# One ring of weight blocks for the last four stages of a hybrid decoder step, the merge's branch products in three passes, and a transposed down projection

## The reference, cut to what matters

```python
h  = RMSNorm(x) * (1 + scale1(c)) + shift1(c)
P  = h @ w_in                      # RWKV-7 group | NSA group | gates gA, gB
yA = RWKV7(P_rwkv) @ w_pa ;  yB = NSA(P_nsa) @ w_pb        # (T, 512) @ (512, 1024)
x  = x + gate1(c) * ((sigmoid(gA) * yA + sigmoid(gB) * yB) @ w_o)
h2 = RMSNorm(x) * (1 + scale2(c)) + shift2(c)
x  = x + gate2(c) * ConvGLU(h2)    # up (1024 -> 2 x 2816), conv of width 3, SiLU, down (2816 -> 1024)
```

## Time and profile before

| | us |
|---|---|
| median of 3 runs (lowest, highest) | 2840.73 (2837.29, 2842.52) |
| the profiled execution, time | 2833.18 |
| the profiled execution, span of its instructions | 2831.5 |
| TensorE busy with matmuls | 2524.0 (89%) |
| VectorE busy | 1179.9 (42%) |
| ScalarE busy | 699.4 (25%) |
| GpSimd busy | 384.2 (14%) |

### The profile page before, as it was taken

How to read it: one execution, slowest core, us unless ns; L and a number is a source line. 1 busy time by engine, 2 the same in 40 slices (tenths; PEclk the granted TensorE clock), 3 DMA queues, 4 the chain that set the end, 5 groups by cost and what they waited for, 6 DMA issues and landing times. The chain is left out here.

```text
span 2831.5 us, 47908 instructions
## 1 busy us (share of the span) xinstructions
PE 2524.0 (89%) x20071; PEld 2054.6 (73%) x20071; DVE 1179.9 (42%) x2457; ACT 699.4 (25%) x1400; POOL 384.2 (14%) x284
## 2 busy tenths in 40 slices
PE   4896998999857898989986999999799999979999
PEld 2675885454434676868585888744799999979999
DVE  5331224555512444435363011134233333359998
ACT  3231124566411213222222000011111111113333
POOL 3001200000120000000002111000222233223320
PEclk6897987999868989999997999999899999989999
DMA  7434411101332000000002101031211111122210
GB/s 266 183 135 133 140 35 43 31 1 46 105 119 76 17 6 24 7 23 3 12 3 102 27 26 31 9 126 55 57 50 49 45 45 45 45 95 73 70 49 16
DMA packets 150472, 171.45 MB, mean 61 GB/s; under 512 B 14089, under 2 KB 135242, under 8 KB 147762
## 3 DMA queue, kind: packets, MB, share of 16 engines
q1 hardware_dynamic: 144626, 152.66, 16.7%
q0 software_dynamic: 5632, 15.74, 1.9%
HBM read 155.47 MB, written 17.05 MB: 61 GB/s over the span
## 5 line engine op out<-in xcount | busy, mean ns | idle before, releaser
L173 PE MATMUL pP_u<-h_hi,w_up_hi 128*128 128x352 f32 x1056 | 341.5, 323 | 11.8 <-POOL w_up_lo L167 11.8
L174 PE MATMUL pP_u<-h_lo,w_up_hi 128*128 128x352 f32 x1056 | 339.2, 321 | 0.0
L175 PE MATMUL pP_u<-h_hi,w_up_lo 128*128 128x352 f32 x1056 | 338.8, 321 | 0.0
L173 PE MATMUL pP_d<-w_down_hi,a_piece_hi 128*128 128x256 f32 x792 | 226.4, 286 | 31.1 <-DVE a_piece_lo L2911 31.1
L174 PE MATMUL pP_d<-w_down_lo,a_piece_hi 128*128 128x256 f32 x792 | 225.3, 284 | 0.0
L175 PE MATMUL pP_d<-w_down_hi,a_piece_lo 128*128 128x256 f32 x792 | 225.1, 284 | 0.0
L173 PEld LDWEIGHTS pP_u<-h_hi,w_up_hi 128*128 128x128 f32 x1056 | 198.8, 188 | 11.9 <-POOL w_up_lo L167 11.9
L174 PEld LDWEIGHTS pP_u<-h_lo,w_up_hi 128*128 128x128 f32 x1056 | 199.0, 188 | 0.0
L175 PEld LDWEIGHTS pP_u<-h_hi,w_up_lo 128*128 128x128 f32 x1056 | 198.5, 188 | 0.0
L1584 PE MATMUL pB_e<-hT,w_rwkv 128*128 128x352 f32 x576 | 182.3, 473 | 16.7 <-DVE rw_slots L1608 9.5
L2801 DVE TENSOR_TENSOR conv<-conv,conv_sig 128x1056 f32<-128x1056 f32 x22 | 50.4, 2289 | 322.8 <-ACT conv_sig L2769 322.8
(11 more groups left out here) (468 smaller groups left out, 4741.5 us busy)
## 6 DMA issues: line engine op xcount, KB each, us to landing
w_up<-in_w_up SPq DMA_DIRECT2D x44, 512.0 KB, 4.1
ybT<-in_w_ada SPq DMA_DIRECT2D x9, 2048.0 KB, 7.6
kv_ring<-in_pool_kv SPq DMA_DIRECT2D x80, 128.0 KB, 2.1
xt<-in_x SPq DMA_DIRECT2D x16, 512.0 KB, 3.7
cx<-in_pool_c POOLq DMA_DIRECT2D x64, 128.0 KB, 3.0
cx<-in_pool_c SPq DMA_DIRECT2D x64, 128.0 KB, 2.9
w_gate<-in_w_in SPq DMA_DIRECT2D x16, 512.0 KB, 4.2
w_rwkv<-in_w_in SPq DMA_DIRECT2D x14, 512.0 KB, 4.1
```

The source lines that it names most:

```text
L173: nc.tensor.matmul(out, w_hi, x_hi, start=start, stop=False)
L174: nc.tensor.matmul(out, w_hi, x_lo, start=False, stop=False)
L175: return nc.tensor.matmul(out, w_lo, x_hi, start=False, stop=stop)
```

## The change

Everything up to the last stage of `rwkv` keeps its instructions; only tiles that `Finish` doesn't use are given back before it.

A ring of weight blocks takes the place of the stages' own weight tiles, from `Finish` to the end: two raw slots of 1024 columns, two slots of high and low parts. The blocks have one numbering: 32 for the merge (gate block, branch block in turn), 44 for the up projection, 24 for the down projection. So the first blocks of a stage are loaded and split in the stage before it.

```diff
+def load_block(sp, S, n, source):
+    if n >= 2:
+        sp.wait_ge(S["w_split"], 2 * (n - 1))
+    rows, width = source.shape[1:]
+    dst = S["w_raw"][:, n % 2, 0:rows * width].rearrange("p (k n) -> p k n", n=width)
+    sp.dma_start(dst, source).then_inc(S["w_in"][n % 2], 16)
+
+def split_block(nc, pool, S, n, size=1024):
+    pool.wait_ge(S["w_in"][n % 2], 16 * (n // 2 + 1))
+    x = slice(0, size)
+    split(nc, nc.gpsimd, S["w_raw"][:, n % 2, x], S["w_hi"][:, n % 2, x], S["w_lo"][:, n % 2, x], S["w_split"], 2 * n)
+
+def block_part(S, n, at):
+    return [S[w][:, n % 2, at:at + 128] for w in ("w_hi", "w_lo")]
+
+UP0, DOWN0 = 32, 32 + 2 * FC
...
+DOWN_Q = 256
+DOWN_PART = [(0, 4), (4, 8), (8, 12), (12, 16), (16, 20), (20, 22)]
```

In `Finish`, SP loads blocks 0 and 1 and POOL splits them. In the merge the branch product is made in three passes too, piece by piece into two PSUM banks, from `y_hi` and `y_lo`, which ScalarE and VectorE make anew in every phase (1408 elements a partition for each piece):

```diff
             @block.gpsimd
             def _(pool):
-                for g in range(16):
-                    pool.wait_ge(wg_in[g % 2], 16 * (g // 2 + 1))
-                    if g >= 2:
-                        pool.wait_ge(mm, 2 * (g - 2) + 1)
-                    split(nc, nc.gpsimd, WG[:, g % 2], WGR[0][:, g % 2], WGR[1][:, g % 2], w_split, 2 * g)
+                for n in range(2, UP0 + 1):
+                    ph, kind = (n - 2) // 2, n % 2
+                    if kind == 0:
+                        pool.wait_ge(gate_mm, ph + 1)
+                    else:
+                        pool.wait_ge(y_mm, 3 * (ph + 1))
+                    split_block(nc, pool, S, n, 1024 if n % 2 == 0 else 512)
...
+                    pe.wait_ge(S["w_split"], 2 * (2 * ph + 2))
                     for i in range(3):
+                        k = 3 * ph + i
+                        if k >= 2:
+                            pe.wait_ge(used, k - 1)
+                        pe.wait_ge(y_split, k + 1)
                         for q in range(4):
-                            last = nc.tensor.matmul(pP[:, 1, i, 0:PIECE], WP[:, w, q, 128 * f:128 * f + 128],
-                                                    y[:, q, i * PIECE:(i + 1) * PIECE], start=(q == 0), stop=(q == 3))
-                    last.then_inc(mm, 1)
+                            last = split_product(nc, pY[:, k % 2, 0:PIECE], block_part(S, 2 * ph + 1, 128 * q),
+                                                 (y_hi[:, i, q, :], y_lo[:, i, q, :]), q == 0, q == 3)
+                        last.then_inc(y_mm, 1)
...
+                        if ph < 15:
+                            low(ph + 1, i)
```

```diff
+                    if k == 0 and h:
+                        pe.wait_ge(evicted, 3 * (h - 1) + i + 1)
                     pe.wait_ge(lo_done, m + 1)
-                    for f in range(b - a):
-                        last = split_product(nc, pP[:, m % 8, 0:Q], [x[:, m % 3, f, :] for x in AR],
-                                             [x[:, n % 3, f, :] for x in WR], f == 0, f == b - a - 1)
-                    last.then_inc(mm, 1)
+                    for half in range(2):
+                        for f in range(b - a):
+                            last = split_product(nc, pP[:, i, half, 0:PIECE], block_part(S, DOWN0 + n, Q * f + 128 * half),
+                                                 [x[:, m % 3, f, :] for x in AR], k == 0 and f == 0, k == NK - 1 and f == b - a - 1)
+                        if half == 1:
+                            last.then_inc(mm, 1)
+                        if turn_after[m, half] is not None:
+                            turn(turn_after[m, half])
+                for r in last_turns:
+                    turn(r)
...
+                for n, (h, k) in enumerate(chunks[1:], 1):
+                    if n == 1:
+                        pool.wait_ge(S["up_mm"], 2 * FC)
+                    else:
+                        pool.wait_ge(mm, 3 * (n - 1))
+                    split_block(nc, pool, S, DOWN0 + n, Q * (PART[k][1] - PART[k][0]))
```

More of the change, by code:

```diff
@@ L1567, in _ @@
                 def _(sp):
+                    for g in range(2):
+                        load_block(sp, S, g, merge_block(A, g))
                     sp.dma_start(O["shift"], R["last"][:, :, :]).then_inc(done, 16)
                     sp.wait_ge(done, 16)
+                @block.gpsimd
+                def _(pool):
+                    for g in range(2):
+                        split_block(nc, pool, S, g, 1024 if g == 0 else 512)
 RW_CHUNKS = [12, 13] + [c for p in range(4) for c in (4 + p, p, 8 + p)]
@@ L2499, in _ @@
             def _(sp):
[L2500 to L2507 removed]
+                for n in range(2, UP0):
+                    load_block(sp, S, n, merge_block(A, n))
@@ L2532, in _ @@
-                    if g == 0:
-                        pe.wait_ge(wp_in, 32)
-                    if g >= 1:
-                        pe.wait_ge(used, g)
-                    y = (S["yaT"], S["ybT"])[w]
+                            last = split_product(nc, pG[:, w, i, 0:PIECE], block_part(S, 2 * ph, 128 * q),
+                                                 (h_hi[:, q, span(i)], h_lo[:, q, span(i)]), q == 0, q == KC - 1)
+                    last.then_inc(gate_mm, 1)
+                    pe.wait_ge(S["w_split"], 2 * (2 * ph + 2))
@@ L2886, in _, with turn @@
             @block.tensor
             def _(pe):
+                def turn(r):
+                    j, (c0, w) = r // 3, CUTS[r % 3]
+                    pe.wait_ge(evicted, j + 1)
+                    if r >= 2:
+                        pe.wait_ge(gated, r - 1)
+                    for half in range(2):
+                        last = nc.tensor.transpose(pT[0:w, r % 2, 128 * half:128 * half + 128], fT[:, j % 3, half, c0:c0 + w], S["ident"])
+                    last.then_inc(turned, 1)
                 for m, (n, i) in enumerate(pieces):
@@ new lines, in _ @@
+                for m, (n, i) in enumerate(pieces):
+                    if m >= 2:
+                        for half in range(2):
+                            if turn_after[m - 2, half] is not None:
+                                output(turn_after[m - 2, half])
+                    a, b = PART[chunks[n][1]]
+                    dve.wait_ge(hi_done, m + 1)
+                    nc.vector.tensor_tensor(AR[1][:, m % 3, 0:b - a, :], aT[:, a:b, PIECE * i:PIECE * i + PIECE],
+                                            AR[0][:, m % 3, 0:b - a, :].bitcast(F32), ALU.subtract).then_inc(lo_done, 1)
@@ L2931, in step_kernel @@
+                for r in last_turns:
+                    output(r)
 def step_kernel(nc, A, OUT):
```

314 lines of the change are left out of this document (169 added, 145 removed).

## The result

The changed kernel takes 2755.49 us (median of 4 runs, 2747.46 to 2765.39) where the kernel before, on the same chip, takes 2841.62 (4 runs, 2837.29 to 2843.26): the ratio is 0.9701, with a 95% interval of 0.9666 to 0.9735. In a second set of runs it took 2753.95 (5 runs) against 2844.26, ratio 0.9684 (0.967 to 0.9699). The forecast was 2757.6, in 2745 to 2780. In the table the last product of `ffn_down` is taken to end where a next one could have started.

The account below looks back on a forecast made before the run. The last four stages were taken as bound by TensorE's own pace, except at the seams. The terms summed to -83.1 us, giving 2750.1 for the profiled execution and 2757.6 from the median, range 2745 to 2780.

Parts of the forecast that it names:

- Parts 1 and 5: Starts of merge and ffn_up: first blocks split earlier, so TensorE starts sooner, -13.3 and -8.2 us.
- Part 2: Merge: branch products as 36 float32r products a phase, 1728 products in all at 159.1 ns, -23.5 us.
- the term for the clock: Start of a stage: first products go at half clock, costing about 1.3 us.
- Part 3: End of the merge: only a third of the width is left for VectorE behind TensorE, -1.5 us.
- Part 4: out_proj: matmuls unchanged, SP's extra loads and POOL's split cost nothing, zero.
- Part 6: Start of ffn_down: no wait for gate rows, but POOL's split holds VectorE's first subtraction, -5.4 us.
- Part 7: ffn_down: 1584 products plus clock, transposes and stalls take 265.2 us instead of 303.9, -38.7 us.
- The stalls: ffn_down: TensorE waits where POOL's splits stand against VectorE's work, taken as 6 us between nothing and 21.5.
- rival A: ffn_down: VectorE and POOL hinder each other at every chunk, 23 splits at 0.9 us, 15.5 more, 2773; chance 0.14.
- the turns: ffn_down: 27 pairs of transposes between the products, 54 at 0.11 us, 5.9 us.
- Part 8: End of the kernel: nine VectorE pairs at 0.9 us stand behind the last product, +7.5 us.
- Rival C: Merge and ffn_down: VectorE locks POOL out, splits come late, 97 us lost against 83, 2855, slower; chance 0.04.

Follow-up runs that it names:

- the repeated profile: The changed kernel unaltered, run and profiled again on the same chip as the kernel before: 2753.95 us, ratio 0.9684.
- the faster version: Changed kernel with w_o in eight earlier loads, SyncE's convolution-store wait dropped, POOL's first ffn_down split after the first low part: 2742.39 us, ratio 0.9648.
- the deeper ring: Kernel before, with ffn_down's a_piece ring five slots deep and output written four tiles behind: 2825.96 us, ratio 0.9933.

## Why the prediction was right, step by step

**Parts 1 and 5, the seams**: -13.2 and -8.7 measured for -13.3 and -8.2 forecast. In `ffn_up` the first product comes 0.32 us behind `h_lo`, not 0.8, and from there to the last `aT` copy the stage was 0.2 us shorter, though nothing in it changed.

**Part 2, branch products**: -22.0 for -23.5. The sigmoids of the first three phases lie at 1543.46, 1560.63 and 1577.80, 17.17 us apart, which is 108 products at 159.0 ns; so pace and count were right, and rows where something waits are missing, as said. What was mis-sized is the term for the clock. From 1529 to 1534.5 the granted clock was 0.50, the lower of the two levels (1.2 GHz), with products 0.29 us apart; that cost 2.7 us, not 1.3. The forecast had sized the term on the shortest such stretch in the table above; over its nine it costs 1.4 to 2.9 us. In the repeated profile the merge's start cost 1.5, and Part 2 comes out at -23.2.

**Part 3**: -1.5 for -1.5. **Part 4, `out_proj`**: I took zero, measured is +1.3 (+0.5 in the repeated profile). In both kernels the first product waits for `w_o`, 12.5 us now and 13.7 before, and both start at the lower clock; 1.0 of the 1.3 is that it lasted longer this time (64 products in 30.5 us, 29.5 before), 0.3 that `w_o` came later after the merge's end.

**Part 6, start of `ffn_down`**: -5.7 for -5.4. POOL's subtraction there does hold VectorE's first: the faster version, in which POOL lets it go first, gains 2.0 us from ScalarE's start to the first product.

**Part 7, products of `ffn_down`**: -40.1 for -38.7. The stalls were 2.1 us as recorded, 2.8 from start to start, where I took 6, and rival A, which needed 21.5, is out. (The 0.9 a split in the forecast is 13.1 over the 14 waits; over the 16 splits named there it would be 0.8.) Of the 3.2 us gained there, the clock (2.1 for 1.3) and the turns (6.5 for 5.9) took back 1.4. A turn of two transposes stands in the timeline of TensorE between two groups of three products:

```profile
2553.18 0.32 PE L173 MATMUL pP_d<-a_piece_hi,w_hi 128*128 128x352 f32 x1
2553.66 0.38 PE L2993 MATMUL pT_d<-cst,f_cols 128*128 128x128 f32 x2
2553.80 0.41 PE L173 MATMUL pP_d<-a_piece_hi,w_hi 128*128 128x352 f32 x1
...
2554.38 0.32 PE L173 MATMUL pP_d<-a_piece_hi,w_hi 128*128 128x352 f32 x1
2554.85 0.33 PE L173 MATMUL pP_d<-a_piece_hi,w_hi 128*128 128x352 f32 x1
```

Three groups take 1.67 us with the pair in between, and 1.43 without (0.477 each): 0.24 us, 0.12 for a transpose, where the forecast had 0.11. The 275 ns that the Trainium skill, page "TensorE: Matmul & The Clock Gate", Part 4 on the transpose, gives for one in bf16 in a kernel would be 0.55 for the pair. The recorded duration of one is near it (0.27 median in float32 here), but among other products it overlaps with them, and what a transpose adds is 0.12.

**Part 8, the end**: +6.8 for +7.5. The nine pairs are seen 0.79 us apart, not 0.9:

```profile
2746.93 0.42 DVE L3028 TENSOR_TENSOR gated_rows<-pT_d,gate_ffn_p 128x256 f32<-128x256 f32 x1 [4.28 <-PE pT_d L2993]
...
2753.28 0.41 DVE L3028 TENSOR_TENSOR gated_rows<-pT_d,gate_ffn_s 96x256 f32<-96x256 f32 x1
2753.73 0.42 DVE L3031 TENSOR_TENSOR x_rows<-gated_rows,x_rows 96x256 f32<-96x256 f32 x1
```

**The sum**: the changed parts make -83.3 (forecast -83.1), but the two profiled spans differ by 75.2 only. Ahead of that point the profile after is 8.1 us longer: 7.1 in the stages before `Finish`, which the change doesn't touch, and 1.0 in `Finish`, which isn't there in the repeated profile. It is scatter: the deeper ring, with the same instructions up to there as the kernel before, has `yaT` done 10.8 us later than that kernel. The forecast had met it with the 7.5 us between the first profile and its median; the medians differ by 86.1. That all terms came within 1.5 us is in part luck, since one term moves by up to 1.4 from profile to profile, and the clock was sized too low in Parts 2 and 7 and the stalls too high; the sum is better than its terms.

**Rival C** fell for the reason given for the phases within the merge. Of its price, no run shows the 4.1 us a phase; for the clock it had 1.3 us a wait, where 1.8 were measured behind waits of 8.4. Its reading of the earlier trace rows, that 24 subtractions without a gap keep POOL out to their end, was right and is now shown from both sides. The rule quoted there from the Trainium skill, page "SBUF — State Buffer", section "SBUF: two separate sides", that the side which starts first holds the ports for its whole instruction, describes the runs in which the two take turns: there one subtraction of VectorE stood for 2.66 us while POOL's of 2.50 ran. The casts of 6.93 and 12.4 us were held through many instructions, which that sentence does not cover; here the measurement goes beyond the page.

## What to carry to other kernels

Put a stage's first weights, load and split, into the stage before, and check on which row of which other engine they would fall otherwise: here the second question was worth as much as the first (17.8 us lost with the loads early and only the splits in the row, 17.8 with both late). Where GpSimd and VectorE share work of a stage, start GpSimd before VectorE's long row of subtractions or not until it is over. And when stalls are taken off TensorE, count them from start to start: here each cost 0.24 us more than the wait that the profile recorded, a quarter on top of the 13.1 us.

## What the runs showed of the hardware beyond that

- VectorE and GpSimd, both on instructions that read and write SBUF in float32, take turns as long as GpSimd asks within the first few instructions of VectorE's row (shown for one and three, and for GpSimd first). After eight instructions back to back, 0.44 us apart, GpSimd's cast was held for the rest of the row: it took 6.93 us where the row had 22 instructions and 12.4 where it had 27, and ended 0.9 us behind the row each time. It did not depend on the tiles, the block of the program, the waits within the row or ScalarE. Why it turns, at which instruction, and whether it is a count or a time, is open.
- While they take turns, both lose: a cast of 1024 columns took up to 2.31 us instead of 1.04, GpSimd's subtraction up to 3.60 instead of 2.34, VectorE's subtraction of 352 columns up to 2.67 instead of 0.51.
- At the start of a stage the lower clock lasted 3.0 to 6.2 us, in two profiles of one kernel 3.1 and 5.7 at the same place. Waits of 8.4 us in the middle of full-clock work cost another 1.8 each, at a granted clock of 0.86; waits of 1.74 us left it at 1.00.
- Weights of 4 MB for `w_o` asked for in eight pieces instead of two halved TensorE's wait for them (12.4 to 6.2 us), though in the same version these loads were also issued ahead of the gate rows; the two were not separated.
